# Residual adds ahead of both weight remainders in the last step of a stage

## The reference, cut to what matters

```python
def rms_norm(x, g):
    y = xf * lax.rsqrt(jnp.mean(xf * xf, axis=-1, keepdims=True) + EPS)
    return (y * g.astype(jnp.float32)).astype(x.dtype)
...
        x = x + o @ w_out[i]
        x = x + memory_cross_attention(rms_norm(x, norm_cross[i]), m, ...)
        x = x + conv_gated_mlp(rms_norm(x, norm_ffn[i]), w_up[i], conv_w[i], conv_b[i], w_down[i])
...
    hx = hx + g1 * yx
    fx = modulate(rms_norm_2(hx, norm_ffn[i]), sh2, sc2)
    hx = hx + g2 * swiglu(fx, ffn_w1[i], ffn_w3[i], ffn_w2[i])
```

## Time and profile before

| | |
|---|---|
| median of 3 runs | 1732.81 us (1732.21 to 1732.85) |
| the profiled execution's own time | 1731.13 us |
| its span | 1729.3 us |
| granted TensorE clock, mean | 0.984 |
| TensorE matmul, busy | 1651.4 us |
| VectorE, busy | 1108.9 us |
| ScalarE, busy | 816.6 us |
| DMA | 293.58 MB, mean 170 GB/s |

### The profile page before, as it was taken

One profiled execution on the slowest core, in us unless ns is written; L12 is line 12 of the kernel. 1 busy time (PEld: TensorE's weight loads), 2 busy tenths in 40 slices (PEclk: granted clock), 3 DMA queues, 4 the chain that ended last, 5 costly groups with the idle time before them and its releaser, 6 DMA issues.

```text
span 1729.3 us, 36156 instructions
## 1 busy us (share of the span) xinstructions
PE 1651.4 (95%) x12468; PEld 1524.8 (88%) x12482; DVE 1108.9 (64%) x1643; ACT 816.6 (47%) x1380; POOL 45.4 (3%) x45
## 2 busy tenths in 40 slices
PE   9989989999998998999989999989999989999998
PEld 7977779999897777999979888878999979989997
DVE  5555668888865556888866454558555664665544
ACT  5556556653444655665355322224544343454443
POOL 2000000000310000000000000000000000000000
PEclk9999999999989999999999999999999999999999
DMA  8430325568555033556935543348455755545551
GB/s 323 147 122 1 122 86 182 182 206 280 205 176 184 1 121 103 185 178 233 373 121 167 174 159 122 131 132 343 143 183 181 249 195 170 169 135 182 182 182 61
DMA packets 81016, 293.58 MB, mean 170 GB/s; under 512 B 9008, under 2 KB 10544, under 8 KB 80176
## 3 DMA queue, kind: packets, MB, share of 16 engines
q1 hardware_dynamic: 78768, 283.29, 48.4%
q10 hardware_dynamic: 2176, 9.27, 1.5%
HBM read 291.48 MB, written 1.05 MB: 169 GB/s over the span
## 4 chain that ended last, share of the span: by engine, by line
PE 80%; DVE 10%; ACT 5%; issue 4%; DVEq 1%; SPq 0%; ACTq 0%; POOL 0%; POOLq 0%
PE projs L1438 48%; PE accs L1438 25%; PE ob L1438 6%; ACT WH L454 3%; DVE WL L862 2%; DVE rstd L949 1%; PE projs L1633 1%; DVE cprod L870 1%; ACT scr L498 1%; DVE scr L955 1%; DVE ring L872 1%; DVE AL L964 1%; DVE x L886 0%; DVE scr L1013 0%; DVE nmax L992 0%
## 5 line engine op out<-in xcount | busy, mean ns | idle before, releaser
L862 DVE TENSOR_TENSOR WL<-ring,WH 128x1024 fp32r<-128x1024 f32 x436 | 543.1, 1247 | 455.5 <-ACT WH L454 454.7
L454 ACT ACTIVATE WH<-ring 128x1024 fp32r (+1 forms) x436 | 460.8, 1057 | 625.4 <-PE projs L1438 327.9
L1438 PE MATMUL projs<-AH,WH 128*128 128x256 f32 (+1 forms) x2304 | 577.8, 290 | 28.2 <-ACT AH L516 9.5
L1438 PE MATMUL projs<-AL,WH 128*128 128x256 f32 (+1 forms) x2304 | 579.7, 291 | 1.3
L1438 PEld LDWEIGHTS projs<-AH,WH 128*128 128x128 f32 x2304 | 439.1, 193 | 40.1 <-issue 19.2
L1438 PEld LDWEIGHTS projs<-AL,WH 128*128 128x128 f32 x2304 | 438.6, 193 | 18.0 <-DVE AL L962 7.1
L1438 PE MATMUL projs<-AH,WL 128*128 128x256 f32 (+1 forms) x2304 | 330.5, 287 | 0.0
L1438 PEld LDWEIGHTS projs<-AH,WL 128*128 128x128 f32 x2304 | 302.4, 193 | 2.5
L1438 PE MATMUL accs<-FH,WH 128*128 (+1 forms) x768 | 186.9, 280 | 0.3
L1438 PE MATMUL accs<-FL,WH 128*128 (+1 forms) x768 | 186.7, 279 | 0.0
L1438 PEld LDWEIGHTS accs<-FH,WH 128*128 128x128 f32 x768 | 144.1, 188 | 1.2 <-issue 1.2
(11 more groups left out here) (235 smaller groups left out, 1742.1 us busy)
## 6 DMA issues: line engine op xcount, KB each, us to landing
ring<-in_stream SPq DMA_DIRECT2D x532, 512.0 KB, 3.4
W1v<-in_w ACTq DMA_DIRECT2D x2, 1024.0 KB, 7.1
W1k<-in_w ACTq DMA_DIRECT2D x2, 1024.0 KB, 10.8
D<-in_decay ACTq DMA_DIRECT2D x4, 512.0 KB, 5.4
x<-in_xT SPq DMA_DIRECT2D x2, 512.0 KB, 5.0
memT<-in_memT SPq DMA_DIRECT2D x1, 1024.0 KB, 11.2
ctxT<-in_ctxT ACTq DMA_DIRECT2D x1, 1024.0 KB, 5.5
out_y<-ybuf SPq DMA_DIRECT2D x8, 128.0 KB, 2.0
```

The lines of the kernel that those rows point to most:

```text
L454: A(WH[:, s, :], ring[:, r % RING, :], ACT.Copy).then_inc(wh_ready, 1)
L862: V.tensor_tensor(WL[:, s, :], ring[:, r % RING, :], WH[:, s, :].bitcast(F32), ALU.subtract).then_inc(consumed, 1)
L1438: return T.matmul(out, lhsT, rhs, start=start, stop=stop, skip_group_check=True)
```

## The change

In the last step of an `into_x` stage VectorE does not make the remainder of the next stage's piece 0 at s = 0. It goes on to s = 1, adds the four banks, and then makes both remainders, of piece 0 and of piece 1, one after the other. In the last stage of the program there is no remainder to make, before or after. The other engines' programs are untouched.

```diff
                     for s in range(2):
-                        if last and s == 1 and into_x:
+                        if last and into_x:
+                            if s == 0:
+                                continue
                             residual(gate)
+                            if k + 1 < len(TABLE):
+                                for half in range(2):
+                                    split(TABLE[k + 1]["r0"] + half, TABLE[k + 1]["p0"] + half, half)
+                            continue
                         if before:
```

## The result

The changed kernel takes 1716.6 us (median of 4 runs, 1716.07 to 1717.21) against 1732.51 for the kernel before, ratio 0.9911, 95% interval 0.9894 to 0.9928. In a second series it took 1718.07 against 1732.03, ratio 0.9926 (0.9912 to 0.9940). The profiled execution has a span of 1714.2 us, 15.1 less than before.

The account below looks back on a forecast made before the run. It took TensorE (95% busy) as the bound, with VectorE's order mattering only at stage ends. Terms 0.4 + 0.9 + 0.3 + 1.1 + 5.6 + 2.1 = 10.4 us off 1732.8 gave 1722.4 us, range 1718.5 to 1727.5.

Parts of the forecast that it names:

- The chain and the adds: At stage ends, piece 0's remainder leaves the way to the adds (1.14 us), so sums and reciprocal come earlier; 10.4 us altogether.
- the nine ends: The ends of all stages but the last, where the remainder moves behind the adds; forecast gains sum to 10.4 us.
- the tight ends: Ends of out, mo (both layers) and co, limited by TensorE: gains 0.4, 0.9 and 0.3 us.
- the loose ends: Ends of f2 of layer 0, down (both layers) and ro, limited by VectorE: adds move by the whole 1.14 us.
- The list of signs: What the new trace should show, such as idle time ahead of the sums: 0.15 us at out, mo, co; 0.4 at f2.
- The clock kept in down of layer 1 and ro: Shorter idle times ahead of their sums keep the full clock: 3.05 + 2.58 = 5.6 us; 2.3 if it falls.
- Down of layer 0: At this stage end 2.99 us of idle time remains, so the clock still falls, for less long: gain 2.1 us.
- R at P + 6.33: Down of layer 0: reciprocal's start (R) after the sums' start (P), taken from ro before the change; was P + 7.24.
- The remainder behind the adds costs nothing: At nine ends the moved 1.14 us fits VectorE's wait before the second remainder, tightest at f2 of layer 0, 0.36 us spare.
- The later load: Ring slot freed some 2.5 us later, so SyncE requests one 512 KB load later; costed at nothing, upper bound 2.5 us.
- Other stretches that are at the lower level now begin elsewhere as all behind moves: Low-clock stretches behind the moved work may shift either way; 2 us allowed each way, within the rival of chance 0.07.
- the second rival's end: Lower end of the rival that it gains more (clock kept in down of layer 0, stretches shift): 1718.8 us, chance 0.07.

Follow-up runs that it names:

- the run that kept the clock behind 2.56 us: The new order only at the ends of out, mo (both layers) and co, the kernel before's order elsewhere: 1724.51 us, ratio 0.9964.
- before_idle1: The kernel before with one idle VectorE operation ahead of the scaled blocks of layer 1's first norm: 1727.92 us, ratio 0.9984.
- after_idle2: The changed kernel with two idle VectorE operations (1.0 us) ahead of the scaled blocks of layer 1's first norm: median 1717.69 us.
- all_but_down0: The changed kernel with the old order at the end of down of layer 0 alone: 1722.60 us, ratio 0.9945.
- Ada_behind: The changed kernel with the last step's modulation pieces also behind the adds, ahead of both remainders (mo keeps the old place): 1714.36 us, ratio 0.9901.
- the three kernels with a forecast from filled gaps in layer 1's mixing: Idle matmuls in mixing gaps of the kernel before (1726.88 us), the changed kernel (1715.07), and the one with modulation pieces behind the adds (8 more matmuls, 1712.91).
- before_filled: The kernel before with idle matmuls: 8 ahead of layer 1's gate logits, 16 ahead of the memory's products in both layers: 1726.88 us, ratio 0.9970.

## Why the prediction was wrong

- *The chain and the adds.* Right. From TensorE's last matmul to the reciprocal, the nine ends gave 11.0 to 11.2 us for 10.4. The sums of the tight ends follow TensorE's last matmul by 0.15 us, and the idle time ahead of them at the loose ends fell by 1.12 to 1.14. The list of signs has about 0.4 us for what is left at f2 of layer 0; the sum's own figures give 1.41 - 1.14 = 0.27, and the trace has 0.29.
- *The clock kept in down of layer 1 and ro.* Right (2.84 and 2.68 for 3.05 and 2.6), with an incomplete reason: the argument was the length of the idle time, 1.7 and 1.4 us; the run that kept the clock behind 2.56 us shows that the place counts as well.
- *Down of layer 0.* Forecast: lost again, R at P + 6.33, 2.1 us. Measured: lost again, P + 5.95, 2.43 us.
- *The remainder behind the adds costs nothing.* Right; room of 0.17 us was left at ro and f2 where 0.36 was forecast. The later load did not show: ScalarE's waits for loads into the ring are 34.8 us in all before and 34.4 after, the longest 3.2 in both.
- *The step that failed.* "Other stretches that are at the lower level now begin elsewhere as all behind moves ... that goes both ways, and I allow 2 us each way", put at zero in the sum and at 0.07 in the chances. It was a term of its own: 3.9 us in layer 1's mixing and attention, twice what was allowed, and with the ends' own 11 it takes the time below the range. (The range's lower bound is called the second rival's end; that is 1718.8, not 1718.5, which changes nothing here.) It is no chance of a single execution (189.8 and 189.7 against 185.6 and 185.7), it is not set free by the adds (half a microsecond of waste, or idle matmuls, bring 3.5 to 4.2 us in the same stretch to the kernel before), and with those matmuls in both kernels it is gone from that stretch (0.2 us between them). The trace of before had the evidence: TensorE's clock at 0.82 and 0.79 in windows that the change does not touch, which I did not list as time that could come back.

What stays open: why a given idle time costs the clock in one place and not in another, why some low stretches begin with no idle time ahead of them, and so how the low stretches distribute over the runs of one kernel. Single runs of the unchanged kernel spread over 7.7 us (1726.2 to 1733.9 over all series). I can read the place in a trace, and could forecast a median from it once (before_idle1), but not in after_idle2, and for all_but_down0 only the total. Ada_behind and the three kernels with a forecast from filled gaps in layer 1's mixing came out 2.4 to 6.9 us slower than forecast. So it is shown that the extra 3.9 us are the clock's and not the adds', but not what sets the clock.

## What to carry to other kernels

At the end of a stage, put on the in-order engine first what the next stage's chain waits for, and let preparations fill the wait behind it; cost the end by the engine that then limits it, which is TensorE's last bank at some ends and VectorE's own queue at others. A change that moves work by some microseconds also moves every later stretch of work against the clock: look for windows with a granted clock below 1 anywhere behind the change, and put that time into the range as a term, not as noise. To tell such a gain from the change's own, compare stretches between the same instructions in both traces, take a second trace of each kernel to see which stretches repeat, and repeat the comparison with idle matmuls in the gaps of both kernels.

## What the runs showed of the hardware that was not expected

- A wasted 0.5 us of VectorE made the whole kernel 3.4 us faster (1727.92 against 1731.29).
- After 2.56 us without a matmul the clock was lost in one kernel (sums 5.35 us) and kept in another (3.72 us) at the same instruction.
- The clock also fell with TensorE hardly waiting: in before_filled two low stretches, at 484.4 and 494.6, began within 1 us of the end of 24 matmuls of 28 columns, with no wait over 0.41 us in the 9 us ahead. Whether those matmuls are the reason was not tried.
- The first 197 us of one and the same order of instructions took 196.5 to 199.8 us in five traces, while the stretches behind repeated within 0.2 us between two executions of one kernel.
